# Levels 4 to 6 of a blocked triangular inverse on 32 or 64 columns a head instead of 128, its transpose written by VectorE's 32x32 transposes, in a decoder-layer kernel

## Chip, cores and metric

One core of a Trainium2 chip. The metric is the device time of one execution in microseconds (us); lower is better. TensorE is called PE in the profile's rows, VectorE DVE, ScalarE ACT, GpSimd POOL.

## What is computed

One layer of a hybrid decoder for 1,024 prompt tokens and 32 sample tokens, in float32 throughout: RMSNorm, one input projection (1024 to 3,592 columns), a gated DeltaNet branch (4 heads of 128) beside a short gated convolution, an output projection, a squared-ReLU MLP of width 4096, a gated embedding and a last norm. The change lies in the DeltaNet branch, in the triangular solve of each chunk of tokens:

```python
kk = jnp.einsum("bhnid,bhnjd->bhnij", k, k)
a_mat = jnp.eye(c, dtype=jnp.float32) + jnp.where(strict, beta[..., :, None] * kk * decay, 0.0)
rhs = jnp.concatenate([v * beta[..., None], k * (beta * jnp.exp(g))[..., None]], axis=-1)
sol = lax.linalg.triangular_solve(a_mat, rhs, left_side=True, lower=True, unit_diagonal=True)
u, w = sol[..., :dv], sol[..., dv:]
qk = jnp.einsum("bhnid,bhnjd->bhnij", q, k) * decay
```

The kernel takes chunks of 128 tokens and forms the inverse of the unit lower triangular 128x128 matrix of each head explicitly.

## The kernel before

**Two kinds of TensorE work in one order.** Every dense product is cut into groups of 352 columns (a third of the 1,056 tokens): 24 matmuls of 128x128 weights by 352 columns in a round-robin of three PSUM banks (`pg`). A product's operands are split into a high and a low part (`fp32r`), so that three matmuls stand for one. In the mixer stage the instructions of the recurrence are threaded between those of the input projection. The table `ORDER` is a list of steps `name chunk level n`: all engines walk the same list; at each step an engine does its share of that step, and TensorE then issues `n` matmuls of the projection (`fill`, line 815; here called **fills**). `vector_work` and `thirds` place VectorE's, ScalarE's and GpSimd's work on the projection (the copy out of a bank at line 1600 or 1744, the split of a weight panel into `w_hi` and `w_lo`, the convolution taps of line 1623, the silu) behind the step in whose fills the group ends. So a step's place in the list decides what each in-order engine has to do ahead of it. 72 fills are one projection unit (three groups of 24); the list holds 1,464 fills before the end and 48 behind it.

**The inverse.** There are eight chunks `c` of 128 tokens, worked in pairs (the even one in buffers 0, the odd in 1). `kk` makes the matrix (VectorE into `AT`), `kq` the query matrix. `b1` to `b4` invert the 16x16 diagonal blocks on VectorE in both, `b4` having GpSimd spread the 32x32 diagonal blocks of the transposed inverse into `XT`, and `turned` transposes it back into `X` (line 1853). Then level 4, 5 and 6 double the block size from 16 to 128, each in two steps: `y` is `LY` (the masked matrix, made by GpSimd) times `X` (line 872), ScalarE copies it out of PSUM; `z` is `XT` times that copy (line 886), and VectorE subtracts it from `X` (line 1858). The transpose is kept up at level 4 by a transpose of the whole `X` (line 1861), and at levels 5 and 6 by a second product (line 890) that is subtracted from `XT` (line 1863). All of these matmuls have 128x128 float32 weights and 128 moving columns; one program matmul of float32 is two records in the trace, so four heads are 8 records.

**After the inverse.** `vturn` turns v (ScalarE scales it out of PSUM), and `into`, `kturn`, `solve`, `update`, `sum`, `norm`, `scale` carry the state. The steps that begin with `s_` do the same for the 32 sample tokens between the first pair and the second. Three of them matter here:

- `s_y`: TensorE waits for `so_copied` 3, ScalarE's copy of the third `s_conv` product; it then multiplies the states with 8 moving columns (line 842), as `s_z` and `s_state` do.
- `s_onorm`: a small norm; ScalarE takes its Ln and Exp.
- `s_put`: the first one waits for `q_act` 13, which is that Ln.

Units 13 to 16 of the projection hold z: where one ends, ScalarE splits a weight panel, loads a table, applies silu (which waits for VectorE's copy of the group) and loads the table back.

## Time and profile before

| | |
|---|---|
| median of 3 runs (lowest to highest) | 1499.04 us (1497.4 to 1499.92) |
| the profiled execution | 1499.39 us, span 1497.6 us |
| TensorE | 98% of the span busy, 9,324 matmul records |
| VectorE, ScalarE, GpSimd | 49%, 32%, 17% |
| mean granted TensorE clock | 0.992 of full |

The span runs from the first to the last instruction; the execution's time has some 1.8 us around it. The mixer stage with the recurrence lies at about 118 to 515 us.

### The profile page before, as it was taken

The numbers are of one execution on the slowest core, as the hardware profiler recorded it, in microseconds if no ns is written. First come the engines' busy times: TensorE is split into PE (matmuls) and PEld (weight loads), VectorE is DVE, ScalarE is ACT, GpSimd is POOL, SyncE is SP. The second block draws the span as 40 slices with busy tenths as digits, with TensorE's granted clock in tenths as the row PEclk, the third lists the DMA queues.
The fourth block names the chain that finished last, engine by engine and source line by source line (L and its number), as shares of the span: only waits on it lengthen the run. The fifth ranks groups of instructions, "written<-read, shape, count | busy, mean of one in ns | idle before, by whom it ended". The sixth has DMA issues, their size and how long they took to land.

```text
span 1497.6 us, 24674 instructions
## 1 busy us (share of the span) xinstructions
PE 1463.6 (98%) x9324; PEld 1437.9 (96%) x9324; DVE 729.3 (49%) x1313; ACT 476.9 (32%) x856; POOL 248.2 (17%) x306
## 2 busy tenths in 40 slices
PE   7999999999999999999999999999999999999997
PEld 6999998999999899999999999999999999998997
DVE  5678844658584733633333333333433333335525
ACT  6324343332424322632131220312213122135525
POOL 3200312154343733000000000000000000040303
PEclk9999999999999999999999999999999999999999
DMA  7112313312213353111111111111111111112102
GB/s 178 44 43 58 99 34 99 92 40 71 72 45 106 64 117 84 32 55 42 42 43 57 43 43 43 54 44 43 43 56 42 43 43 56 43 42 72 29 29 116
DMA packets 166315, 89.83 MB, mean 60 GB/s; under 512 B 50763, under 2 KB 160267, under 8 KB 166230
## 3 DMA queue, kind: packets, MB, share of 16 engines
q1 hardware_dynamic: 165222, 84.89, 20.6%
q0 software_dynamic: 1008, 3.79, 0.6%
q8 instruction: 55, 0.90, 0.2%
q14 instruction: 30, 0.25, 0.1%
HBM read 77.97 MB, written 10.69 MB: 59 GB/s over the span
## 4 chain that ended last, share of the span: by engine, by line
PE 89%; DVE 4%; issue 2%; POOL 1%; ACT 1%; DMA 0%; DVEq 0%; POOLq 0%; SPq 0%
PE pg L696 65%; PE pg L815 14%; PE bk L872 1%; DVE act_lo L1975 1%; PE bk L890 1%; PE bk L886 1%; POOL act_lo L2296 1%; PE bk L842 1%; PE bk L1023 1%; DVE cv L1623 0%; PE bk L856 0%; PE bk L903 0%; PE bk L935 0%; PE bk L923 0%; PE bk L932 0%
## 5 line engine op out<-in xcount | busy, mean ns | idle before, releaser
L696 PE MATMUL pg<-act_hi,w_hi 128*128 128x352 f32 x1320 | 428.3, 325 | 8.0 <-issue 3.5
L696 PE MATMUL pg<-act_lo,w_hi 128*128 128x352 f32 x1320 | 424.5, 322 | 0.0
L696 PE MATMUL pg<-act_hi,w_lo 128*128 128x352 f32 x1296 | 416.1, 321 | 0.0
L696 PEld LDWEIGHTS pg<-act_hi,w_hi 128*128 128x128 f32 x1320 | 248.6, 188 | 11.1 <-issue 7.2
L696 PE MATMUL pg<-u_hi,w_hi 128*128 128x352 f32 x768 | 249.3, 325 | 0.0
L696 PEld LDWEIGHTS pg<-act_lo,w_hi 128*128 128x128 f32 x1320 | 249.2, 189 | 0.0
L696 PE MATMUL pg<-u_hi,w_lo 128*128 128x352 f32 x768 | 248.9, 324 | 0.0
L696 PE MATMUL pg<-u_lo,w_hi 128*128 128x352 f32 x768 | 247.8, 323 | 0.0
L696 PEld LDWEIGHTS pg<-act_hi,w_lo 128*128 128x128 f32 x1296 | 243.5, 188 | 0.0
L1152 ACT ACTIVATE w_hi<-w_raw 128x1024 fp32r<-128x1024 f32 x111 | 117.0, 1054 | 383.2 <-PE pg L696 319.8
L2337 POOL TENSOR_TENSOR ssq<-ssq,sq 128x352 f32<-128x352 f32 x72 | 76.2, 1067 | 875.3 <-ACT sq L1152 874.6
L2036 DVE TENSOR_TENSOR xres<-xres,pg 128x352 f32 (+1 forms) x192 | 99.2, 520 | 201.0 <-PE pg L696 201.0
L815 PE MATMUL pg<-act_hi,w_hi 128*128 128x352 f32 x504 | 167.1, 332 | 2.6 <-DVE pre L1600 2.6
L1543 DVE TENSOR_TENSOR w_lo<-w_raw,w_hi 128x1024 fp32r<-128x1024 f32 x110 | 138.6, 1260 | 58.4 <-ACT w_hi L1152 58.2
L815 PE MATMUL pg<-act_hi,w_lo 128*128 128x352 f32 x504 | 166.2, 330 | 0.0
L815 PE MATMUL pg<-act_lo,w_hi 128*128 128x352 f32 x504 | 165.5, 328 | 0.0
L696 PEld LDWEIGHTS pg<-u_hi,w_hi 128*128 128x128 f32 x768 | 145.0, 189 | 0.0
L696 PEld LDWEIGHTS pg<-u_lo,w_hi 128*128 128x128 f32 x768 | 144.5, 188 | 0.0
L696 PEld LDWEIGHTS pg<-u_hi,w_lo 128*128 128x128 f32 x768 | 143.9, 187 | 0.0
L1152 ACT ACTIVATE sq<-tm 128x352 f32<-128x352 f32 x96 | 47.8, 498 | 231.6 <-DVE tm L2022 231.6
L2026 DVE TENSOR_TENSOR u_lo<-sq,u_hi 128x352 f32 x96 | 50.5, 526 | 129.8 <-ACT u_hi L1152 129.8
L815 PEld LDWEIGHTS pg<-act_hi,w_hi 128*128 128x128 f32 x504 | 95.9, 190 | 5.4 <-DVE pre L1600 2.9
(331 smaller groups left out, 1643.8 us busy)
## 6 DMA issues: line engine op xcount, KB each, us to landing
w_raw<-in_w_up SPq DMA_DIRECT2D x32, 512.0 KB, 4.0
w_raw<-in_w_down SPq DMA_DIRECT2D x32, 512.0 KB, 3.4
w_raw<-in_w_in SPq DMA_DIRECT2D x29, 512.0 KB, 4.1
x_tok<-in_x_prompt SPq DMA_DIRECT2D x8, 512.0 KB, 8.0
w_raw<-in_w_out SPq DMA_DIRECT2D x8, 512.0 KB, 4.3
x_col<-in_x_prompt SPq DMA_DIRECT2D x32, 128.0 KB, 2.8
w_raw<-in_w_ple_gate SPq DMA_DIRECT2D x8, 512.0 KB, 4.1
out<-y_tok SPq DMA_DIRECT2D x8, 512.0 KB, 2.9
```

What stands on the lines that cost most here:

```text
L696: last = mm(pg[bank][:, 0:TH], w, a, start=i == 0, stop=i == len(terms) - 1)
L815: last = mm(pg[n][:, 0:TH], w, (act_hi, act_lo, act_hi)[r][:, k, cols(n)], start=k == 0 and r == 0, stop=k == KD - 1 and r == 2)
L842: last = mm(bk[4][:, c:c + 8], S_in[:, h, i, :], F0[:, c:c + 8], start=True, stop=True)
L872: per_head(lambda h, v: mm(A[x][:, v], LY[x][:, h, :], X[x][:, h, :], start=True, stop=True)) \
L886: last = per_head(lambda h, v: mm(A[x][:, v], XT[s][x][:, h, :], LY[x][:, h, :], start=True, stop=True))
L890: last = per_head(lambda h, v: mm(bank[:, v], LY[x][:, h, :], XT[s][x][:, h, :], start=True, stop=True))
L1023: mm(bk[c % 4][:, :], F0[0:TS, c // 2 * P:(c // 2 + 1) * P], by_seq[c % 4][0:TS, :, :], start=True, stop=True).then_inc(sm.q_pe, 1)
L1152: return nc.scalar.activation(out, in_, func, **kw)
L1543: tt(w_lo[b % 2][:, :, :], w_raw[b % 2][:, :, :], w_hi[b % 2][:, :, :].bitcast(f32), SUB) \
L2026: tt(rows(u_lo[c % 2][:, k, cols(n)]), sq[g % 2][:, :], rows(u_hi[c % 2][:, k, cols(n)]).bitcast(f32), SUB).then_inc(sm.u_lo_made, 1)
L2036: tt(x_t, x_t, pg[g % 3][:, 0:TH], ADD).then_inc(sm.evacuated, 2)
L2337: tt(ssq[:, cols(n)], ssq[:, cols(n)], sq[g % 2][:, :], ADD).then_inc(sm.ssq_added, 1)
```

## The change

The inverse is no longer held as a full 128x128 square for each head. At level 4 and 5 only its diagonal 32x32 blocks (32 columns a head, `narrow`) are multiplied, at level 6 its 64x64 blocks (64 columns a head, `pairs`). So `y` and `z` keep their 128x128 weights (`LY`, `XT`) and move 32 or 64 columns. The second product of levels 5 and 6 is gone: the new blocks of the transposed inverse are written straight into `XT` by VectorE's 32x32 block transposes, at level 6 after ScalarE has negated the product. Level 6 has one product before and after. The `turned` step is replaced by one transpose in `b4`. The masked matrix of the next level is made by GpSimd after `y` instead of after `z`, the rows of the next pair are loaded after `y` of level 6, and the fill counts in `ORDER` are all new; their sum is the same.

```diff
@@ z, y and kq on TensorE @@
                 elif k == "kq":
...
-                    if c > 1:
-                        pe.wait_ge(sm.x_updated, upd(c // 2 * 2 - 1, SQUARE))
...
                 elif k == "y":
                     pe.wait_ge(sm.lt_made, lev(c, l))
                     if l == BASE:
-                        pe.wait_ge(sm.x_copied, c + 1)
+                        pe.wait_ge(sm.x_copied, c // 2 + 1)
                     else:
-                        pe.wait_ge(sm.x_updated, upd(c, l - 1, l - 1 < SQUARE))
-                    per_head(lambda h, v: mm(A[x][:, v], LY[x][:, h, :], X[x][:, h, :], start=True, stop=True)) \
+                        pe.wait_ge(sm.x_updated, upd(c, l - 1, 1 if l == BASE + 1 else 2))
+                    src = pairs(x) if l == LEVELS - 1 else narrow(x)
+                    out = columns(A[x][:, half_cols(l)[0]], wide(l))
+                    per_head(lambda h, v: mm(out[:, h, :], LY[x][:, h, :], src[:, h, :], start=True, stop=True)) \
                         .then_inc(sm.y_mm, 1)
                 elif k == "z":
...
-                    if l < LEVELS - 1:
-                        last = per_head(lambda h, v: mm(A[x][:, v], XT[s][x][:, h, :], LY[x][:, h, :],
-                                                        start=True, stop=True))
-                    if l >= SQUARE:
-                        bank = A[2] if l == SQUARE else A[x]
-                        last = per_head(lambda h, v: mm(bank[:, v], LY[x][:, h, :], XT[s][x][:, h, :],
-                                                        start=True, stop=True))
-                    last.then_inc(sm.z_mm, 1)
+                    src = y_copy(x, l)
+                    out = columns(A[x][:, half_cols(l)[1]], wide(l))
+                    per_head(lambda h, v: mm(out[:, h, :], XT[s][x][:, h, :], src[:, h, :], start=True, stop=True)) \
+                        .then_inc(sm.z_mm, 1)
@@ ScalarE @@
                 elif k == "y":
                     act.wait_ge(sm.y_mm, lev(c, l))
-                    op(LY[x][:, :, :], heads(A[x]), ACT.Copy).then_inc(sm.ycopy_made, 1)
+                    if l == LEVELS - 1:
+                        act.wait_ge(sm.x_updated, upd(c, l - 1))
+                    op(y_copy(x, l), columns(A[x][:, half_cols(l)[0]], wide(l)), ACT.Copy).then_inc(sm.ycopy_made, 1)
+                elif k == "z" and l == LEVELS - 1:
+                    act.wait_ge(sm.z_mm, lev(c, l))
+                    op(negated(x)[64:P], A[x][64:P, half_cols(l)[1]].rearrange("p (a b j) -> p a b j", a=2, b=2), ACT.Copy, scale=-1.0) \
+                        .then_inc(sm.c_negated, 1)
@@ VectorE @@
+                    nc.vector.transpose(X[0][:, 0:2, :], X[1][:, 0:2, :]).then_inc(sm.x_copied, 1)
-                elif k == "turned":
-                    dve.wait_ge(sm.xt_made, c + 1)
-                    nc.vector.transpose(flat(X[x]), flat(XT[s][x])).then_inc(sm.x_copied, 1)
                 elif k == "z":
-                    xt = XT[s][x]
-                    dve.wait_ge(sm.z_mm, lev(c, l))
+                    xt, low, both = XT[s][x], narrow(x), pairs(x)
                     if l < LEVELS - 1:
-                        tt(X[x][:, :, :], X[x][:, :, :], heads(A[x]), SUB).then_inc(sm.x_updated, 1)
-                    if l < SQUARE:
-                        dve.wait_ge(sm.x_updated, upd(c, l, False))
-                        nc.vector.transpose(flat(xt), flat(X[x])).then_inc(sm.x_updated, 1)
+                        dve.wait_ge(sm.z_mm, lev(c, l))
+                        product = columns(A[x][:, half_cols(l)[1]], wide(l))
+                    if l == BASE:
+                        tt(low, low, product, SUB).then_inc(sm.x_updated, 1)
+                        dve.wait_ge(sm.x_updated, upd(c, l, 1))
+                        for g in range(GROUPS):
+                            f = slice(32 * g, 32 * g + 32)
+                            nc.vector.transpose(xt[f, :, f], low[f]).then_inc(sm.x_updated, 1)
+                    elif l == BASE + 1:
+                        dve.wait_ge(sm.xt_made, c // 2 * 2 + 2)
+                        stt(both[:, :, 0:32], low, m_grp[:, GROUPS:GROUPS + 1], product, MUL, SUB).then_inc(sm.x_updated, 1)
+                        ts_(both[:, :, 32:64], low, m_grp[:, GROUPS + 1:GROUPS + 2], None, MUL).then_inc(sm.x_updated, 1)
+                        dve.wait_ge(sm.x_updated, upd(c, l, 2))
+                        for g in (0, 2):
+                            f = slice(32 * g, 32 * g + 32)
+                            n = slice(32 * g + 32, 32 * g + 64)
+                            nc.vector.transpose(xt[f, :, n], both[n, :, 0:32]).then_inc(sm.x_updated, 1)
                     else:
-                        tt(xt[:, :, :], xt[:, :, :], heads(A[2] if l == SQUARE else A[x]), SUB).then_inc(sm.x_updated, 1)
+                        dve.wait_ge(sm.c_negated, c + 1)
+                        for g in range(2):
+                            for j in range(2):
+                                f = slice(32 * j, 32 * j + 32)
+                                n = slice(64 + 32 * g, 96 + 32 * g)
+                                nc.vector.transpose(xt[f, :, n].rearrange("p (a b) j -> p a b j", a=2), negated(x)[n, :, :, f]) \
+                                    .then_inc(sm.x_updated, 1)
@@ the order table, one line of it @@
-y 0 5 9; y 1 5 0; z 0 5 34; z 1 5 26; y 0 6 18; y 1 6 0; z 0 6 18; z 1 6 7;
+y 0 5 25; y 1 5 20; z 0 5 0; z 1 5 15; y 0 6 5; y 1 6 19; z 0 6 0; z 1 6 33;
```

**TensorE, levels 5 and 6 of the second pair.** Before (line 872 is y, 886 and 890 the two products of z, 912 `kturn`, 923 and 831 `solve` with the old state, 932 `update`; `bk` is a PSUM bank of the recurrence, `pg` one of the fills):

```order
L872 MATMUL bk<-X,LY 128x128 x4
L912 MATMUL bk<-ident,qkv 128x128 x4
L886 MATMUL bk<-LY,XT 128x128 x4
L890 MATMUL bk<-XT,LY 128x128 x4
L815 MATMUL pg<-act_lo,w_hi 128x352
L815 MATMUL pg<-act_hi,w_lo 128x352
L923 MATMUL bk<-rv,XT 128x128 x4
L831 MATMUL bk<-qkv,S 128x128 x4
L886 MATMUL bk<-LY,XT 128x128 x4
L890 MATMUL bk<-XT,LY 128x128 x4
L932 MATMUL bk<-wn,ktok 128x128 x4
L872 MATMUL bk<-X,LY 128x128 x4
```

After (893 is y, 903 z, 935 and 852 `solve`, 944 `update`):

```order
L893 MATMUL bk<-X,LY 128x32 x4
L903 MATMUL bk<-X,XT 128x32 x4
L935 MATMUL bk<-rv,XT 128x128 x4
L852 MATMUL bk<-qkv,S 128x128 x4
L903 MATMUL bk<-X,XT 128x32 x4
L836 MATMUL pg<-act_hi,w_lo 128x352
L836 MATMUL pg<-act_hi,w_hi 128x352
L836 MATMUL pg<-act_lo,w_hi 128x352
L836 MATMUL pg<-act_hi,w_lo 128x352
L944 MATMUL bk<-wn,ktok 128x128 x4
```

A z of level 5 is 4 matmuls of 32 columns now, and was 8 of 128.

**ScalarE, the sample steps up to s_y.** `X<-bk 27x512` is the copy of the second `s_conv` product, `PT<-bk 27x512` here that of the third, `w_hi`, the two table loads and `cv<-cv` the work at the end of a z unit, `PT<-bk 32x128` the copy in `s_y`. Before:

```order
L1152 ACTIVATE X<-bk 27x512
L1152 ACTIVATE X<-bk 32x128
L1152 ACTIVATE PT<-bk 27x512
L1152 ACTIVATE PT<-bk 32x128
L1152 ACTIVATE w_hi<-w_raw 128x1024
L1152 ACT_TABLE_LOAD
L1152 ACTIVATE cv<-cv 128x1056
L1220 ACT_TABLE_LOAD
L1152 ACTIVATE PT<-bk 32x512
L1152 ACTIVATE LY<-LY 128x128
L1152 ACTIVATE LY<-bk,eps 128x128
L1152 ACTIVATE LY<-LY 128x128
```

After, from the same copy on:

```order
L1164 ACTIVATE X<-bk 27x512
L1164 ACTIVATE X<-bk 32x128
L1164 ACTIVATE w_hi<-w_raw 128x1024
L1164 ACT_TABLE_LOAD
L1164 ACTIVATE cv<-cv 128x1056
L1232 ACT_TABLE_LOAD
L1164 ACTIVATE PT<-bk 27x512
L1164 ACTIVATE PT<-bk 32x128
L1164 ACTIVATE PT<-bk 32x512
L1164 ACTIVATE LY<-LY 128x128
```

The unit's work stood behind the third copy and stands ahead of it. TensorE has 12 fills between the third `s_conv` and `s_y` now, 8 before. The fills of these two pieces are in the table: before `s_conv 2 8; s_y 8`, after `s_xt 9; s_conv 2 12; s_y 10`.

**ScalarE, the norm and the first s_put.** `LY<-bk,eps` is the Ln of `s_onorm`. In the piece of before it directly follows the square `LY<-LY`. After:

```order
L1164 ACTIVATE LY<-LY 128x128
L1164 ACTIVATE w_hi<-w_raw 128x1024
L1164 ACT_TABLE_LOAD
L1164 ACTIVATE cv<-cv 128x1056
L1232 ACT_TABLE_LOAD
L1164 ACTIVATE LY<-bk,eps 128x128
```

The next z unit's end has moved ahead of the Ln. The fills: before `s_solve 29; s_out 0; s_onorm 26; s_put 0`, after `s_solve 18; s_out 15; s_onorm 17; s_put 0`.

## Rows read from the trace of the kernel before

**Rows 1.** The page: span, TensorE's share, the chain that ended last by engine.

```profile
span 1497.6 us, 24674 instructions
PE 1463.6 (98%) x9324; PEld 1437.9 (96%) x9324; DVE 729.3 (49%) x1313; ACT 476.9 (32%) x856; POOL 248.2 (17%) x306
...
PE 89%; DVE 4%; issue 2%; POOL 1%; ACT 1%; DMA 0%; DVEq 0%; POOLq 0%; SPq 0%
```

**Rows 2.** Windows: busy us of each engine (instructions), PEclk granted, DMA share, GB/s.

```profile
282.00:507.00 225.00, 224.78 (x1615) 220.50 (x1614) 150.96 (x335) 80.56 (x179) 96.58 (x91) 1.00 0.24 67
163.50:166.80 3.30, 3.30 (x13) 3.30 (x13) 3.30 (x7) 0.00 (x0) 3.30 (x4) 0.50 0.00 0
228.30:231.70 3.40, 3.40 (x37) 3.34 (x36) 0.36 (x1) 2.77 (x3) 0.60 (x1) 1.00 0.55 140
231.75:238.45 6.70, 6.70 (x29) 6.36 (x29) 0.67 (x5) 0.59 (x1) 0.00 (x0) 0.50 0.21 85
```

**Rows 3.** Who ended TensorE's waits, 120 to 520 us: total us, times, longest.

```profile
PE pg L815 <- DVE pre L1600: 2.6, 1, 2.6
...
PE bk L856 <- issue: 1.5, 1, 1.5
PE bk L1015 <- ACT LY L1152: 1.0, 1, 1.0
PE bk L959 <- ACT X L1152: 0.6, 1, 0.6
PE bk L864 <- issue: 0.2, 1, 0.2
```

**Rows 4.** TensorE's timeline in the second pair: start us, us, operands, records.

```profile
313.03 1.05 PE L872 MATMUL bk<-X,LY 128*128 128x128 f32 x8
313.92 0.60 PE L912 MATMUL bk<-ident,qkv 128*128 128x128 f32 x4
314.36 1.06 PE L886 MATMUL bk<-LY,XT 128*128 128x128 f32 x8
315.25 1.06 PE L890 MATMUL bk<-XT,LY 128*128 128x128 f32 x8
316.06 0.41 PE L815 MATMUL pg<-act_lo,w_hi 128*128 128x352 f32 x1
```

**Rows 5.** TensorE's timeline around s_y.

```profile
223.58 0.33 PE L815 MATMUL pg<-act_lo,w_hi 128*128 128x352 f32 x1
223.74 1.85 PE L842 MATMUL bk<-LY,S_in 128*128 128x8 f32 x16
225.52 0.43 PE L983 MATMUL bk<-X,AT 32*32 32x32 f32 x8
225.88 0.43 PE L815 MATMUL pg<-act_hi,w_lo 128*128 128x352 f32 x1
```

**Rows 6.** VectorE's timeline at the end of b3 and b4.

```profile
159.86 0.69 DVE L1776 TENSOR_REDUCE W<-X 128x64 f32<-128x512 f32 x1
160.58 0.74 DVE L1848 TENSOR_SCALAR X<-W,m_half 128x256 f32<-128x256 f32 x2
161.36 1.03 DVE L1849 STREAM_TRANSPOSE X<-X 128x512 f32<-128x512 f32 x1
162.49 0.53 DVE L1600 TENSOR_TENSOR pre<-pg,r_b 128x352 f32<-128x352 f32 x1
```

**Rows 7.** ScalarE's timeline: third s_conv copy, a z unit's end, the Ln.

```profile
222.65 0.59 ACT L1152 ACTIVATE PT<-bk 27x512 f32<-27x512 f32 x1 [0.62 <-PE bk L959]
...
226.34 1.06 ACT L1152 ACTIVATE w_hi<-w_raw 128x1024 fp32r<-128x1024 f32 x1
227.42 1.28 ACT L1152 ACT_TABLE_LOAD   x1
228.71 1.08 ACT L1152 ACTIVATE cv<-cv 128x1056 f32<-128x1056 f32 x1
229.81 1.28 ACT L1220 ACT_TABLE_LOAD   x1
...
247.33 0.37 ACT L1152 ACTIVATE LY<-bk,eps 128x128 f32<-128x128 f32 x1 [0.58 <-PE bk L1015]
```

**Rows 8.** VectorE's timeline from s_out on.

```profile
246.33 4.62 DVE L1954 TENSOR_TENSOR S_in<-S_in,XT 128x1024 f32<-128x1024 f32 x4
250.87 0.28 DVE L1958 TENSOR_TENSOR qkv<-LY 128x128 f32<-128x128 f32 x1
251.11 0.52 DVE L1744 TENSOR_TENSOR cv<-pg,r_b 128x352 f32<-128x352 f32 x1
```

**Rows 9.** TensorE's timeline at s_out and s_onorm.

```profile
244.69 1.07 PE L1010 MATMUL bk<-XT,AT 32*128 32x32 f32 x8
246.81 0.49 PE L1015 MATMUL bk<-LY,ones 128*128 128x128 f32 x2 [1.05 <-ACT LY L1152]
247.05 0.41 PE L815 MATMUL pg<-act_lo,w_hi 128*128 128x352 f32 x1
```

More of the change, by code:

```diff
@@ L76 @@
-norm 7 0 0; scale 7 0 0; tail 0 0 0
+begin 0 0 0; diff 0 0 8; diff 1 0 0; kk 0 0 79; kk 1 0 38; b1 0 0 17; b2 0 0 22; kq 0 0 44; b3 0 0 0; kq 1 0 5;
+b4 0 0 50; y 0 4 0; y 1 4 7; z 0 4 4; z 1 4 35; y 0 5 25; y 1 5 20; z 0 5 0; z 1 5 15; y 0 6 5; y 1 6 19;
+z 0 6 0; z 1 6 33; s_wait 0 0 0; s_begin 0 0 42; s_norm 0 0 17; s_conv 0 0 0; s_kk 0 0 18; s_conv 1 0 0;
+s_xt 0 0 9; s_conv 2 0 12; s_y 0 0 10; s_z 0 0 0; s_state 0 0 6; s_turn 0 0 4; s_solve 0 0 18; s_out 0 0 15;
+s_onorm 0 0 17; s_put 0 0 0; s_put 1 0 8; s_put 2 0 0; s_put 3 0 10; s_put 4 0 0; s_put 5 0 11; s_put 6 0 0;
@@ new lines @@
+s_put 7 0 45; vturn 0 0 0; vturn 1 0 0; diff 2 0 0; diff 3 0 3; kk 2 0 0; kq 2 0 0; kk 3 0 0; into 0 0 29;
+kq 3 0 0; b1 2 0 11; b2 2 0 20; kturn 0 0 18; b3 2 0 0; solve 0 0 33; b4 2 0 0; update 0 0 0; sum 0 0 14;
+y 2 4 0; y 3 4 0; into 1 0 0; z 2 4 0; z 3 4 16; norm 0 0 12; y 2 5 0; kturn 1 0 3; y 3 5 0; z 2 5 0;
+solve 1 0 0; z 3 5 4; update 1 0 9; sum 1 0 9; y 2 6 2; y 3 6 0; norm 1 0 0; scale 0 0 0; scale 1 0 7; z 2 6 0;
+z 3 6 10; vturn 2 0 13; diff 4 0 0; vturn 3 0 0; diff 5 0 0; kk 4 0 35; kk 5 0 0; kq 4 0 17; into 2 0 0;
@@ new lines @@
+kq 5 0 0; b1 4 0 22; b2 4 0 0; kturn 2 0 8; b3 4 0 2; solve 2 0 32; b4 4 0 0; update 2 0 0; sum 2 0 13;
+y 4 4 0; y 5 4 0; into 3 0 0; z 4 4 0; z 5 4 11; norm 2 0 5; y 4 5 5; kturn 3 0 0; y 5 5 0; z 4 5 0;
+solve 3 0 0; z 5 5 3; update 3 0 8; sum 3 0 2; y 4 6 0; y 5 6 11; norm 3 0 0; scale 2 0 0; scale 3 0 0;
+z 4 6 21; z 5 6 17; vturn 4 0 0; vturn 5 0 0; diff 6 0 0; diff 7 0 18; kk 6 0 0; kk 7 0 0; kturn 4 0 36;
+into 4 0 0; b1 6 0 21; solve 4 0 0; kq 6 0 0; b2 6 0 32; update 4 0 0; sum 4 0 0; kq 7 0 0; b3 6 0 0;
@@ L77 @@
+b4 6 0 27; into 5 0 0; norm 4 0 20; y 6 4 0; y 7 4 0; kturn 5 0 0; z 6 4 25; z 7 4 23; solve 5 0 6; y 6 5 0;
+y 7 5 0; update 5 0 0; z 6 5 0; z 7 5 23; sum 5 0 0; y 6 6 0; y 7 6 18; norm 5 0 0; scale 4 0 0; scale 5 0 6;
+z 6 6 0; z 7 6 21; vturn 6 0 0; vturn 7 0 0; into 6 0 11; kturn 6 0 5; solve 6 0 2; update 6 0 0; sum 6 0 13;
+into 7 0 0; kturn 7 0 0; norm 6 0 13; solve 7 0 17; update 7 0 0; sum 7 0 0; scale 6 0 34; norm 7 0 0;
+scale 7 0 0; tail 0 0 0
 """
@@ L500, in lev, with upd, wide, half_cols @@
             return 2 * (LEVELS - BASE) * (c // 2) + 2 * (l - BASE) + c % 2 + 1
-        def upd(c, l, both=True):
-            pair = 4 * (SQUARE - BASE + 1) + 2
-            if l == LEVELS - 1:
-                return pair * (c // 2) + pair - 2 + c % 2 + 1
-            return pair * (c // 2) + 4 * (l - BASE) + 2 * (c % 2) + (2 if both else 1)
+        def upd(c, l, part=None):
+            parts = {4: 5, 5: 4, 6: 4}
+            first = sum(2 * parts[j] for j in range(BASE, l)) + parts[l] * (c % 2)
+            return 2 * sum(parts.values()) * (c // 2) + first + (part or parts[l])
+        def wide(l):
+            return 64 if l == LEVELS - 1 else 32
+        def half_cols(l):
+            w = H * wide(l)
+            y = 256 if l == BASE + 1 else 0
+            return slice(y, y + w), slice(y + w, y + 2 * w)
+        def narrow(x):
+            return X[0][:, x, :].rearrange("p (h j) -> p h j", h=H)
+        def pairs(x):
+            return X[1][:, 2 * x:2 * x + 2, :].rearrange("p a (b j) -> p (a b) j", b=2)
+        def y_copy(x, l):
+            return pairs(x) if l == LEVELS - 1 else X[0][:, 2 + x, :].rearrange("p (h j) -> p h j", h=H)
+        def negated(x):
+            return view(X[0], P * x, (2 * P, 2), (64, 2), (1, 64))
+        def columns(ap, w):
+            return ap.rearrange("p (h j) -> p h j", j=w)
         def view(buf, offset, *dims):
@@ L628, in _ @@
                         .then_inc(sm.ge_in, 16)
[L629 to L630 removed]
+                elif k == "y" and l == LEVELS - 1 and 2 <= c < NTT - 2:
+                    sp.wait_ge(sm.y_mm, lev(c, l))
                     load_rows(c + 2)
```

44 lines of the change are left out of this document (10 added, 34 removed).

## Prediction

> **What bounds the kernel.** I read the page first: the span, TensorE's share of it, and the chain that ended last. TensorE is busy for 98% of the span and holds 89% of the chain [rows 1]. A part of the change is therefore worth what it does to TensorE's own queue, and an operation of another engine costs nothing until TensorE waits for it. The windows come next. From 282 to 507 us, where three of the four pairs are worked, TensorE is busy for 224.78 of 225 us at the full clock; VectorE has 33% to spare there, ScalarE 64% [rows 2]. The list of waits then says how little TensorE waits between 120 and 520 us: 2.6 us once for a bank that VectorE had not copied out, 1.5 us for `kk` 2, 1.0 at `s_onorm`, 0.6 at the third `s_conv`, 0.2 at a `kq` [rows 3]. Two stretches in that region run at the half clock, 3.4 and 6.8 us long [rows 2]. So there are three accounts: TensorE's work, its waits, and the clock.
>
> **1. TensorE's work.** What does a narrow matmul cost? With 128 moving columns the 8 records of line 872 start at 313.03 and the next group at 313.92: 0.89 us, 111 ns a record; lines 886 and 890 the same [rows 4]. With 8 moving columns on 128x128 weights, 16 records take 223.74 to 225.52: again 111 ns [rows 5]. The weights are what these two rows share, so the moving columns are free below 128, and all of `y` and `z` keep their 128x128 weights. I take 111 ns for 32 and 64 columns. The lower bound is the next row: 32x32 weights, 8 records in 0.36 us, 45 ns [rows 5]; it needs narrow weights, which this change doesn't have.
>
> The Trainium skill has a rule that speaks for a larger gain: in "TensorE: Matmul & The Clock Gate", section "Back-to-back issue gap", a matmul of 1 to 64 columns costs about 60 cycles, or 62 ns where the sequencer decodes. By that the 384 remaining records would each be some 50 ns cheaper, an estimate of 19 us more. The 8-column row disagrees, and the same page's section on LDWEIGHTS, where the time goes by weight columns, is with the row.
>
> What does go is the second product of level 5: 8 chunks x 4 heads x 2 records = 64 records x 111 ns = **-7.1 us**. The other groups stay, 24 `y` and 24 `z`, and the sum of fills is unchanged.
>
> **2. The wait at 160 us.** TensorE stands 2.6 us for a bank because `b3` and `b4` keep VectorE until 162.49, and only then is the group copied out [rows 3, 6]. Behind the wait the clock is halved: 13 records start in 3.3 us where 160 ns each would need 2.1, so 1.2 us more are lost [rows 2, 5]. The new table brings `kk` 0 forward to fill 8 and puts `b3` at fill 208, behind the group that ends at fill 192. The next group ends at fill 216 and its bank is asked for at fill 264: 48 fills, 7.7 us, while VectorE has what is left of `b3` and `b4`, about 5 us. The bank is free in time: **-3.8 us** (bounds: 0 if VectorE is as late elsewhere, -4.3 if the whole half-clock stretch, half of 3.4, is counted).
>
> **3. Waits that go.** `s_conv` 2 now has 9 fills (1.4 us) ahead of it: -0.6. `s_onorm` has 15 (2.4 us) after `s_out`: -1.0. The `kq` wait of 0.2 goes too. Together **-1.8 us** [rows 3]. The 1.5 us at `kk` 2 stay: `vturn` stands 20 fills instead of 13 behind the unit's end, but 3 fills instead of 10 follow it.
>
> **4. Waits that come.** Both are ScalarE's in-order queue around the end of a z unit. That block is 226.34 to 231.09: panel split, table, silu, table, 4.75 us [rows 7].
>
> *At `s_y`.* Before, the third copy stood ahead of it; now it stands behind. The block starts 0.46 us after the unit's last fill has started (225.88 and 226.34) [rows 5, 7], so the copy of 0.59 is done 5.8 us after that fill, a little later for the two copies ahead. TensorE needs 9 fills, `s_conv` 2 and 12 fills, 1.45 + 0.45 + 1.95 = 3.85 us. It waits **+2.1 us**. Queued behind the wait are the state products and all fills; nothing else runs on TensorE.
>
> *At the first `s_put`.* It waits for the Ln, which now stands behind the next block; and the silu in that block waits for VectorE's copy of the group, which stands behind four multiplications of `S_in`. From the start of `s_out` (244.69): those begin at +1.64 and end at +6.2, the group's copy at +6.6 [rows 8, 9]; silu 1.08, table 1.28, Ln 0.37 [rows 7] give +9.4. TensorE is there after 0.9 + 15 fills + 0.25 + 17 fills and two switches, +6.5. **+2.9 us** (bounds for both waits together: 0, if something in my order is off, to 6.5).
>
> **5. The clock.** Two rows show what precedes a fall: a wait of 2.6 us [rows 3], and 3.4 us of 8-column records without a pause [rows 2]. The new wait at `s_y` is followed by 1.8 us of 8-column records, so I expect one more half-clock stretch, over 10 fills: +1.5. The wait at `s_put` is like the one at 160 us: 1.2 us at perhaps three in four, +1.0. Together **+2.5 us** (bounds 0 and 3.4, two stretches at half of 3.4 each).
>
> **6. At no cost.** VectorE does one subtraction of 128 columns and four transposes at level 4 for two operations of 512, similar at 5 and 6; ScalarE gains a negation at level 6. I went through every step from the second pair on, with the fills between a product and its reader. The tightest are `update` 2 (about 0.6 us to spare after `b3`) and `norm` 6 (0.3 us). They are hidden by fills; if the cover is gone in all of them, it costs 1 to 2 us. After level 6 of chunk 3, `vturn` 2 waits for a negation and four transposes, some 1.5 us, and has 10 fills.
>
> **Sum.** 1499.4 - 7.1 - 3.8 - 1.8 + 2.1 + 2.9 + 2.5 = **1494.2 us**. The profiled execution is 1499.39, 0.35 above the median of the runs, which I leave inside the range.
>
> **Rivals.**
>
> *A, the sum above (0.58).* Its own range 1491 to 1497.5, by the clock's and `s_put`'s bounds.
>
> *B, the two ScalarE waits don't appear (0.14).* Something in the sample steps is late already and covers them, with the clock's part. Then -12.7 us alone, 1486.7; with one of them 1490. Against: the order of ScalarE's rows and the duration of the block are both plain.
>
> *C, narrow matmuls let the clock fall, a little (0.20).* A record of 32 columns lies between 8 columns, behind 3.4 us of which the clock was halved [rows 2], and 128, of which any number ran at full clock (282 to 507). The table puts four groups of 32 columns close together in four places, with one of 128 between (level 4 of each pair: y, y, into, z, z), some 4.5 us each. Each fall costs 1.2 to 1.7 us, since all around is TensorE's bound. Two to four falls: 1497 to 1501. The same page of the Trainium skill, section "HAM oscillation", has kernels with short matmul bursts fall to the half clock again and again; this trace shows it for 8 columns and pauses alone.
>
> *D, the same, in more than five places, level 6 too (0.05).* From five falls on, 1494.2 + 5 x 1.6 = 1502.2, slower than before; at all eight level stretches 1507. Against: the clock would have to fall although 128-wide groups and fills stand between.
>
> *E, a narrow matmul is cheaper (0.03).* At 45 ns a record, 384 x 66 ns = 25 us less: 1469.
>
> **How the numbers follow.** 0.2% is 3.0 us, about what a measurement of this kernel tells from no change; faster means under 1496.0. A lies under that by nine tenths (0.52), B and E wholly (0.17): 0.69. C and the rest of A make 0.26 for no change, D 0.05. The range leaves out E, D and the lower half of B: 1489 to 1500.
>
> **What would show it.** The forms of TensorE: y and z at 111 ns a record from start to start, 384 of them; the wait for `pre` at 160 us gone; a wait of 2 us ahead of line 863's first group and of 3 us ahead of the first `s_put`, both ended by ScalarE; PEclk 1.00 from the second pair on. A clock under 1 between 290 and 500 us speaks for C or D. What would make it wrong: VectorE late at a place that I took as covered, or a pace of narrow records that isn't 111 ns.

## The result and the profile after

The changed kernel takes **1506.34 us** (median of 19 runs, 1500.85 to 1511.12) against 1498.82 us (median of 19, 1496.52 to 1507.88) of the kernel before on the same chip: ratio **1.0038, 95% interval 1.0026 to 1.0050**. The prediction was 1494.2 in a range of 1489 to 1500, and faster. It was wrong in sign and outside its range. The profiled execution took 1505.23 us.

The page of the kernel after: span, busy time, the chain by engine. They answer to [rows 1].

```profile
span 1503.5 us, 24634 instructions
PE 1465.2 (97%) x9260; PEld 1435.9 (96%) x9260; DVE 738.2 (49%) x1375; ACT 472.5 (31%) x864; POOL 247.1 (16%) x306
...
PE 91%; DVE 2%; issue 2%; POOL 1%; ACT 1%; DMA 0%; DVEq 0%; POOLq 0%; SPq 0%
```

The trace has 64 TensorE records fewer, as it should, and yet TensorE is busy for 1.6 us more: some of its records take longer. The chain is still TensorE's. The waits of the mixer, 110 to 520 us, against [rows 3]:

```profile
PE bk L1035 <- issue: 3.0, 1, 3.0
PE bk L863 <- ACT PT L1164: 1.9, 1, 1.9
PE bk L877 <- issue: 1.5, 1, 1.5
PE pg L1064 <- POOL act_lo L2332: 1.1, 1, 1.1
```

Line 1035 is the first `s_put`, 863 the state product of `s_y`, 877 `kk` 2. The waits at 160 us, at the third `s_conv`, at `s_onorm` and at `kq` are gone; the two that were forecast have come, at 3.0 and 1.9 us. The windows, against [rows 2] (columns as there):

```profile
163.50:166.80 3.30, 3.30 (x27) 3.30 (x26) 3.27 (x3) 0.60 (x3) 2.87 (x4) 1.00 0.02 5
207.90:224.00 16.10, 14.16 (x110) 12.95 (x108) 4.45 (x13) 8.02 (x14) 2.80 (x6) 1.00 0.30 99
224.10:244.50 20.40, 20.40 (x99) 19.42 (x99) 1.19 (x6) 0.85 (x2) 0.00 (x0) 0.50 0.10 26
244.55:258.10 13.55, 10.53 (x68) 9.79 (x66) 8.53 (x11) 5.63 (x7) 4.62 (x5) 1.00 0.06 9
258.25:271.75 13.50, 13.50 (x27) 7.44 (x26) 3.52 (x6) 0.00 (x0) 4.12 (x4) 0.50 0.48 149
290.00:510.00 220.00, 220.00 (x1569) 215.92 (x1568) 156.99 (x391) 77.08 (x185) 94.44 (x91) 1.00 0.25 68
```

Here is the loss. Half clock of 3.4 us at 163 is gone, but 20.5 us stand from 224.1 to 244.5 and 13.7 from 258.2 to 271.8: 34.1 us at the half clock in the mixer, against 3.4 + 6.8 = 10.2 before. TensorE has no pause in either stretch (20.40 of 20.40 us, 13.50 of 13.50), and from 290 us on, among all the narrow products of the other three pairs, the clock is full.

TensorE's timeline at the start of the two stretches:

```profile
220.71 0.32 PE L836 MATMUL pg<-act_lo,w_hi 128*128 128x352 f32 x1
222.97 2.55 PE L863 MATMUL bk<-LY,S_in 128*128 128x8 f32 x16 [1.94 <-ACT PT L1164]
225.45 0.63 PE L995 MATMUL bk<-X,AT 32*32 32x32 f32 x8
226.01 0.66 PE L836 MATMUL pg<-act_hi,w_lo 128*128 128x352 f32 x1
...
229.11 3.42 PE L863 MATMUL bk<-LY,S_in 128*128 128x8 f32 x16
...
254.59 0.32 PE L836 MATMUL pg<-act_hi,w_lo 128*128 128x352 f32 x1
257.93 1.79 PE L1035 MATMUL bk<-AT,LY 32*128 32x512 f32 x2 [3.02 <-issue]
259.51 1.91 PE L1035 MATMUL bk<-X,LY 32*128 32x512 f32 x2
```

Each fall of this profile comes within 1.2 us of the end of a wait, and what follows the wait is lean: 16 records of 8 columns, or `s_put` products that use 32 of the 128 rows. 16 records of 8 columns take 3.42 us at the half clock and 1.85 at the full one [rows 5]; two `s_put` records start 1.6 to 1.9 us ahead of the next two, against 0.96 at full clock (245.54 and 246.50 in spread_products, a run of below). ScalarE's timeline ahead of both waits:

```profile
217.48 1.04 ACT L1164 ACTIVATE w_hi<-w_raw 128x1024 fp32r<-128x1024 f32 x1
218.54 1.28 ACT L1164 ACT_TABLE_LOAD   x1
219.84 1.09 ACT L1164 ACTIVATE cv<-cv 128x1056 f32<-128x1056 f32 x1
220.94 1.28 ACT L1232 ACT_TABLE_LOAD   x1
222.24 0.59 ACT L1164 ACTIVATE PT<-bk 27x512 f32<-27x512 f32 x1
...
255.06 1.08 ACT L1164 ACTIVATE cv<-cv 128x1056 f32<-128x1056 f32 x1 [0.87 <-DVE cv L1764]
256.17 1.28 ACT L1232 ACT_TABLE_LOAD   x1
257.46 0.37 ACT L1164 ACTIVATE LY<-bk,eps 128x128 f32<-128x128 f32 x1
```

The copy that `s_y` needs (222.24) and the Ln that `s_put` needs (257.46) both stand behind a z unit's block, as the order had it. Line 1035's releaser is printed as "issue"; the Ln that it waits for ends at 257.83, 0.1 us before it starts. And the narrow products in the second pair, against [rows 4]:

```profile
314.24 1.87 PE L893 MATMUL bk<-X,LY 128*128 128x32 f32 x16
315.94 1.14 PE L915 MATMUL bk<-S,qkv 128*128 128x128 f32 x8
316.92 1.87 PE L903 MATMUL bk<-X,XT 128*128 128x32 f32 x16
```

16 records of 32 columns take 1.70 us from start to the next group's start: 106 ns each, where 128 columns took 111.

### The profile page after: what moved, and what is told of

Its sections match the earlier page's. It is cut to its first block, busy times and chain, and to the rows that moved or that the text cites. A ratio compares the mean times of both kernels' runs of the same rounds, so it can differ in the third digit from the quotient of the medians.

```text
span 1503.5 us, 24634 instructions
## 1 busy us (share of the span) xinstructions
PE 1465.2 (97%) x9260; PEld 1435.9 (96%) x9260; DVE 738.2 (49%) x1375; ACT 472.5 (31%) x864; POOL 247.1 (16%) x306
## 4 chain that ended last, share of the span: by engine, by line
PE 91%; DVE 2%; issue 2%; POOL 1%; ACT 1%; DMA 0%; DVEq 0%; POOLq 0%; SPq 0%
PE pg L717 65%; PE pg L836 15%; PE bk L903 1%; PE bk L893 1%; DVE act_lo L2011 1%; PE bk L863 1%; PE bk L1035 1%; POOL act_lo L2332 1%; PE bk L877 0%; PE bk L935 0%; PE bk L883 0%; PE bk L915 0%; PE bk L944 0%; PE bk L947 0%; PE bk L952 0%
```

## What every run tells of the clock

Each run comes with its mean granted clock, so its time can be split: (1 - mean clock) x time is what the clock took, the rest is work and waits at full clock. Means over all runs of a kernel; those of the kernel before are the ones taken beside the experiments. The last column is the half clock between 110 and 500 us in the profiled execution (of two, where there are two).

| kernel | runs | clock took | the rest | half clock, us |
|---|---|---|---|---|
| before | 88 | 13.8 | 1487.0 | 10.2; 10.2 |
| after | 19 | 24.7 | 1481.5 | 34.1; 34.1 |
| old_sample_fills | 6 | 16.7 | 1477.4 | 17.1 |
| before_new_sample | 6 | 22.2 | 1490.6 | 27.3 |
| no_sy_wait | 10 | 19.5 | 1479.8 | 20.5 |
| no_sput_wait | 10 | 18.7 | 1479.0 | 23.9 |
| code_alone | 12 | 19.9 | 1483.4 | 23.9; 17.1 |
| first_pair_alone | 12 | 15.9 | 1489.1 | 10.2 |
| spread_products | 12 | 14.6 | 1477.9 | 0; 0 |
| wait_in_fills | 7 | 13.9 | 1480.1 | 17.1 |
| put_spread | 12 | 25.2 | 1480.3 | 44.4 |
| spread_more | 6 | 11.5 | 1481.1 | 3.4 |
| spread_and_cover | 6 | 10.2 | 1481.3 | 3.4 |
| onorm_cover | 12 | 13.7 | 1476.5 | 13.7 |

The standard error of a mean in the third column is 0.3 for the kernel before, 0.6 for that after, and 0.6 to 2.0 for the others. So the change took 5.5 us out of work and waits and put 10.9 into the clock. The 19 runs of the kernel before that stand beside the changed kernel's 19 come without clocks and can't be split; their mean is 1499.5 us, against 1500.8 in this table, so one of the two terms may be off by about 1 us.

## The experiments

The theory, called W below: the two new waits start half clocks, and the lean work behind them (8-column or 32-row products) holds the clock down. The first rival, N: the narrow products of the inverse leave the clock prone to fall, wherever. The 8-column products of `s_y`, `s_z` and `s_state` are called the state products. All edits are in the table of fills, whose sum stays the same; spread_products, spread_more, spread_and_cover and onorm_cover also let fills in between the state products, by an edit of the code.

**old_sample_fills**: the changed kernel with the sample steps' fills of before. Both waits go.

```diff
-s_begin 42; s_norm 17; s_conv0 0; s_kk 18; s_xt 9; s_conv2 12; s_y 10; s_state 6; s_turn 4; s_solve 18; s_out 15; s_onorm 17; s_put 0 8 0 10 0 11 0 45
+s_begin 16; s_norm 14; s_conv0 14; s_kk 25; s_xt 0; s_conv2 8; s_y 8; s_state 8; s_turn 5; s_solve 29; s_out 0; s_onorm 26; s_put 0 9 0 10 0 16 0 54
```

> The changed kernel with the sample steps' fills at the places of the kernel before (s_norm at fill 442, s_y at 503, s_out and s_onorm at 553, the first s_put at 579). Theory W (waits, then a held half clock): the two ScalarE waits of 1.9 and 3.0 us go, the 1.0 and 0.6 us of the kernel before come back, and the half clock between 210 and 290 us shrinks from 34 us to about 7: some 1505.2 - 3.3 - 12 = 1490 us, ratio to before 0.994. Rival N (the narrow matmuls ahead of the sample steps leave the clock prone to fall): the waits go but 15 to 30 us of half clock stay: 1498 to 1502. Rival O (waits alone, the clock stretches are by chance of the profiled run): 1502 in the median.

Measured: 1494.33 us (6 runs), ratio 0.9954 (0.9937 to 0.9971). The work and the waits came out as summed: -7.1 (records) -2.6 (the wait at 160) = -9.7 against before, 1487.0 - 1477.4 = 9.6 measured, with a standard error of 0.8. (That it fits to a tenth is luck: wait_in_fills, the same kernel but for 13 fills, gives 6.9.) The clock gave back 8.0 of its 10.9. But W had some 7 us of half clock in the sample steps and 1490 us, and the profile has 17.1 us there, as much as N asked for, in the state products, though no wait above 0.6 us is near:

```profile
221.40:238.30 16.90, 16.90 (x80) 15.92 (x80) 1.89 (x6) 4.50 (x5) 0.60 (x1) 0.50 0.21 65
238.50:262.00 23.50, 22.45 (x115) 17.52 (x114) 13.65 (x20) 5.70 (x7) 8.65 (x9) 1.00 0.33 99
```

So a wait is not needed for a fall in that stretch. The second row holds all of `s_put` but its end, without the wait: full clock.

**before_new_sample**: the kernel before with the changed kernel's sample fills, the same edit the other way round (`s_begin` 43, the last `s_put` 38).

> The kernel before, with its 128-wide inverse untouched, and the sample steps' fills at the places of the changed kernel. Theory W: waits of about 2 and 3 us come, and with them 25 to 35 us of half clock between 210 and 290 us: before + 13 to 17 us, ratio 1.009 to 1.011. Rival N: the waits come, but the half clock stays at 7 to 12 us, ratio 1.002 to 1.004.

Measured: 1512.28 us (6 runs), ratio 1.0081 (1.0064 to 1.0097). No narrow product is in it, and it has the same two waits (1.9 and 3.0 us), half clocks of 3.4 and 6.8 us in the state products and of 13.7 behind the wait at `s_put`:

```profile
238.10:244.80 6.70, 6.70 (x30) 6.36 (x30) 0.67 (x5) 0.13 (x1) 0.00 (x0) 0.50 0.00 0
258.60:272.20 13.60, 13.11 (x26) 7.44 (x26) 3.57 (x6) 0.69 (x3) 4.12 (x4) 0.50 0.49 144
```

Its clock took 8.4 us more than before. W had asked for a little more (a ratio of 1.009 to 1.011), N for much less (1.002 to 1.004). N is not the main cause: the fills of the sample steps are. They bring 8.4 of the 10.9 us without any of the changed code.

**no_sy_wait** and **no_sput_wait**: the changed kernel with one wait taken away each, by moving the step to the other side of the z unit's end.

```diff
 no_sy_wait
-s_kk 18; s_xt 9; s_conv2 12; s_y 10
+s_kk 10; s_xt 0; s_conv2 8; s_y 31
 no_sput_wait
-s_solve 18; s_out 15; s_onorm 17
+s_solve 9; s_out 0; s_onorm 41
```

> The changed kernel with s_xt, the third s_conv and s_y ahead of the unit's end at fill 504 (fills s_kk 10, s_xt 0, s_conv 2 8, s_y 31), nothing else moved. Theory W: the wait of 1.9 us is gone, the half clock before 250 us is 7 to 10 us instead of 20, the wait at the first s_put with its 13.7 us stays: about 1505.2 - 1.9 - 5 = 1498. Rival N: 1503, with the 20 us of half clock in place.

> The changed kernel with s_out and s_onorm ahead of the unit's end at fill 576 (fills s_solve 9, s_out 0, s_onorm 41), nothing else moved. Theory W: the wait of 3.0 us is gone, that of 1.0 at s_onorm is back, no half clock after 255 us, the first stretch of 20 us as before: about 1505.2 - 2.0 - 5.5 = 1498. Rival N: the second half-clock stretch stays, 1503.

Measured: 1499.38 (10 runs), ratio 0.9993 (0.9978 to 1.0008), and 1497.57 (10 runs), ratio 0.9982 (0.9969 to 0.9996). Without the first wait the clock took 5.2 us less than after, without the second 5.9 less (standard error about 1 each). Their windows, no_sy_wait first:

```profile
229.60:236.20 6.60, 6.60 (x28) 5.83 (x28) 0.67 (x5) 0.59 (x1) 0.00 (x0) 0.50 0.00 0
250.00:263.50 13.50, 13.50 (x27) 7.59 (x27) 3.57 (x6) 0.06 (x1) 4.12 (x4) 0.50 0.48 153
```

```profile
222.90:229.50 6.60, 6.60 (x34) 6.51 (x34) 0.53 (x1) 0.27 (x1) 0.00 (x0) 0.50 0.45 123
233.10:246.60 13.50, 13.50 (x55) 11.76 (x54) 2.19 (x8) 0.59 (x1) 2.19 (x3) 0.50 0.01 1
250.20:253.50 3.30, 3.30 (x13) 3.30 (x12) 2.93 (x4) 0.00 (x0) 0.00 (x0) 0.50 0.00 0
```

With the wait at `s_put` there are 13.7 us of half clock behind it; without it the `s_put` products run at full clock (the first starts at 257.22); the 3.4 us at 250 us lie among fills, behind a wait of 1.0 us at `s_onorm`.

**code_alone**: the changed code on the table of before, the `turned` steps' fills given to the step ahead.

> The changed kernel's code with the fill counts of before (the two turned steps of each pair dropped, their fills given to the step ahead). It separates the code from the table. If the sums of the prediction hold, TensorE loses 64 records of 111 ns, and the waits of before stay (2.6 us at 160 us with 3.4 us of half clock behind, 1.5 at kk 2, 1.0 at s_onorm, 0.6 at the third s_conv): 1498.8 - 7.1 = 1491.7 us, ratio 0.9953, and about 10 us of half clock between 110 and 520 us as in before. If the narrow products themselves make the clock prone to fall, there are more half-clock stretches in the mixer than before has, some of them in the inverse, and the time is 1495 or more. If the gain of the sample fills in the earlier experiment (ratio 0.9954) came with the new first pair (-3.8), this kernel should be 3.8 us slower than -10.9 would give; if the first pair is worth nothing, it equals that experiment, 1494.

Measured: 1503.35 us (12 runs), ratio 1.0014 (1.0002 to 1.0026). A miss by 12 us. The profile has new waits: 2.8 us at `vturn`, whose VectorE work had more fills ahead of it in the new table, 0.7 at `update`, 0.3 more at 160 us. -7.1 + 3.8 = -3.3; measured in the rest, -3.6. The narrow code needs its own table. The clock took 6.1 more than before, of which the half clock of 3.4 us behind the wait at `vturn` explains 1.7 in this profile.

**first_pair_alone**: the kernel before with the first pair's steps up to `b4` at the new places, the two `turned` steps at fill 243.

> The kernel before, with the first pair's steps from the start to b4 at the changed kernel's fills (kk 0 at fill 8, b3 at 208; the two turned steps behind b4). It tests the second term of the sum by itself: the wait of 2.6 us at 160 us and the 3.4 us of half clock behind it go, y 0 starts 3.8 us earlier (at about 164.6 us instead of 168.4), everything behind it is the same: 1495.0 us, ratio 0.9975. Rival: the later part of the mixer gets its time back at another wait, then 1498.8 with y 0 early all the same; or the clock takes it back in the sample steps, then a half clock longer than 6.8 us there.

Measured: 1504.10 us (12 runs), ratio 1.0026 (1.0010 to 1.0043). A miss by 9 us. The wait at 160 us went, but the old `turned` step waits for GpSimd's part of `b4`, and y 0 for it:

```profile
171.54 3.53 PE L872 MATMUL bk<-X,LY 128*128 128x128 f32 x16 [5.41 <-DVE X L1853]
174.83 0.41 PE L815 MATMUL pg<-act_hi,w_lo 128*128 128x352 f32 x1
```

So the new first pair leans on the new code, which writes that transpose within `b4`, and this kernel does not test the term alone. In old_sample_fills it stands beside the term for the records, and the two together come out. What this row is good for: a wait of 5.4 us, longer than any of after, with 128-column products and fills behind it, cost one half clock of 3.4 us (171.3 to 174.7).

**spread_products**: old_sample_fills with 8 fills between `s_z` and `s_state` and 8 between the latter's two halves.

```diff
-                    against_state(2)
+                    against_state(2)
+                    fill(a, a + 8)
+                    a += 8
                     against_state(3).then_inc(sm.q_pe, 1)
```

> The changed kernel with the sample steps' fills of before (the experiment that measured ratio 0.9954), and 16 more fills between the 8-column state products: 8 ahead of the products of s_state, 8 between its two halves, so that no 32 records of 8 columns stand together; the 16 are taken from behind the last s_put. Same work. If the half clock of 17.1 us that this stretch had in that experiment comes from the 8-column records that stand together, it is gone or at most 3.4 us long: -5 us or so against that experiment, 1489 us, ratio 0.992. If a lean mix is enough, or if it comes from something else (the pause of 0.5 us at the third s_conv, the small products of s_conv and s_kk ahead), the half clock stays and is longer, since more fills are in the stretch at half pace: 1494 to 1497.

**spread_again** is a second profile of it.

> The kernel of spread_products once more, for a second profile of it: its twelve runs fell in two groups, 1484 to 1489 us at a clock of 0.993 to 0.994 and 1495 to 1500 us at 0.985 to 0.989, and the profile shows one of the first. If the second group is a half clock in the sample steps that comes in some executions, a profile of 1495 us or more shows it there, 17 us or longer. If it lies elsewhere (the MLP, the end), the sample steps stay at full clock in it.

Measured: 1492.43 us (12 runs, 1484.29 to 1500.11), ratio 0.9940 (0.9917 to 0.9963); spread_again 1486.24. The runs fall in two groups: six at 1484.3 to 1489.5 with a clock of 0.993 or 0.994, six at 1495.4 to 1500.1 with 0.985 to 0.989. The median is not at the 1489 us that was expected, and the mean of what the clock took, 14.6 against 16.7 in old_sample_fills, differs by about its error. Both profiles are of the first group, and have no half clock in the sample steps at all (spread_again); no profile caught the second group:

```profile
205.00:270.00 65.00, 61.91 (x409) 54.01 (x408) 25.98 (x60) 24.48 (x39) 12.87 (x17) 1.00 0.34 102
```

**spread_more** (halves of 8 records with 6 fills behind each, 48 in all) and **spread_and_cover** (7 fills behind each `s_put` too, `kk` 2 ten fills later):

> The changed kernel with the sample steps' fills of before, and the 8-column state products in halves of 8 records with 6 fills behind each half (48 fills in that stretch, which had 32 when 16 records stood together and 16 in the version before that), taken from behind the last s_put. The experiment with 32 fills had two outcomes, six runs at a mean clock of 0.993 to 0.994 and six at 0.985 to 0.989. If records of 8 columns standing together make the falls, the lower outcome goes: all runs at 0.992 or more, 1487 to 1490 us, ratio 0.9915. If any lean stretch will do and more fills in it only make it longer, both outcomes stay, 1487 and 1497 us.

> The kernel of spread_more with the s_put products evened out too (7 fills behind each) and kk 2 ten fills later behind vturn (they are taken from behind into 0), so that its wait of 1.5 us goes. If the state products were all that made the falls in the sample steps, it is 1.5 us faster than spread_more, 1486 to 1488 us; if the s_put products share in them, the mean clock rises a little more; if kk 2 is the start of a chain (b1, b2) that is needed in time, its wait comes back at y of level 4 and nothing is gained.

Measured: 1492.77 (6 runs), ratio 0.9946 (0.9928 to 0.9964), and 1490.78 (6 runs), 0.9939 (0.9921 to 0.9957). The clock was 0.990 or more in all twelve runs, and what the clock took is the least of all, 11.5 and 10.2. The medians are some 3 us above the ranges that were expected. The gain against spread_products went into a wait: `s_onorm` has moved 32 fills and now stands behind a z unit's block, 2.7 us instead of 1.0, with one half clock of 3.4 us behind it (spread_more: the wait, then the window). In spread_and_cover the 1.5 us at `kk` 2 are gone, and 0.6 came at the `kq` behind it.

```profile
PE bk L1030 <- ACT LY L1167: 2.7, 1, 2.7
```

```profile
244.80:248.00 3.20, 3.20 (x13) 3.20 (x13) 3.20 (x2) 0.68 (x2) 3.20 (x3) 0.50 0.43 168
```

**onorm_cover**: spread_more with that wait taken away (`s_turn` 3, `s_solve` 14, `s_out` 6, so that the step stands ahead of the unit's end).

> The kernel of spread_more with 14 fills instead of 29 between s_solve and s_out and 6 instead of none behind s_out, so that s_onorm stands ahead of the z unit's end and has a cover; kk 2 is five fills later. The wait of 2.7 us at s_onorm (ended by ScalarE) and the 3.4 us of half clock behind it go if ScalarE's block was what it waited for: -2.7 - 1.7 against spread_more, 1488.5 us, ratio 0.992. If VectorE's part behind s_solve is late now, the wait moves to s_out and nothing is gained.

Measured: **1488.59 us** (12 runs, 1482.77 to 1501.32), ratio **0.9930 (0.9901 to 0.9958)**: the lowest median, 1488.5 was expected. The wait is gone. But the two groups are back: six runs at 0.994 or 0.995 (to 1486.15 us), six at 0.983 to 0.990 (from 1491.03 us). The median lies in the gap between them, so that it met the expectation is in part luck, and its interval overlaps those of the three kernels above. Its profile is of the second group:

```profile
205.00:227.10 22.10, 21.55 (x178) 20.70 (x176) 4.97 (x14) 10.22 (x17) 3.57 (x7) 1.00 0.30 87
227.30:240.80 13.50, 13.50 (x55) 13.07 (x54) 1.21 (x7) 0.47 (x1) 0.00 (x0) 0.50 0.05 22
241.00:270.00 29.00, 29.00 (x148) 22.44 (x148) 17.02 (x24) 8.25 (x10) 8.69 (x9) 1.00 0.34 100
```

In the 22.1 us ahead of that fall TensorE paused for 0.55 us in all. With 6 fills between 8 records of 8 columns a fall can still come, and once it had come it lasted for 13.7 us. The Trainium skill, "TensorE: Matmul & The Clock Gate", section "HAM oscillation — how this bites in real kernels", lays the falls that it describes to pauses between bursts of matmuls; this fall and that of old_sample_fills came without such a pause.

**put_spread**: the changed kernel, 9 fills behind each `s_put` instead of none and some by turns. The wait ahead stays.

> The changed kernel with nothing but the fills between the eight s_put products evened out: 9 behind each (11 behind the last) instead of none and 8 to 11 by turns, so that two 32-row products no longer stand together. The first of them stays where it is and so does the wait of 3.0 us ahead of it. If lean work behind a wait holds the half clock, the 13.7 us stretch behind that wait is shorter, 3.4 to 6.8 us: -3.5 to -5 us against the changed kernel, ratio to before about 1.001. If a half clock begun by such a wait has its length from the wait alone, the stretch stays 13.7 us and the ratio 1.0038.

Measured: 1506.17 us (12 runs), ratio 1.0028 (1.0010 to 1.0047), the clock took 25.2. A miss: the stretch behind the wait is not shorter but longer. The windows of both stretches, then the fifth of the eight `s_put` products:

```profile
225.30:249.00 23.70, 23.70 (x109) 22.18 (x110) 2.47 (x8) 0.85 (x2) 1.78 (x2) 0.50 0.09 23
259.50:279.80 20.30, 19.52 (x44) 12.20 (x44) 4.09 (x7) 0.97 (x3) 4.12 (x4) 0.50 0.32 93
```

```profile
279.96 1.12 PE L1035 MATMUL bk<-AT,LY 32*128 32x512 f32 x2
```

Evening out did not end the half clock sooner: it lasted for 20.5 us, through four products and their fills. But it ended at 279.8 us, and the other four products, with the same 9 fills between them, ran at full clock to 289 us. So the mix alone does not hold the clock down for as long as it lasts.

**wait_in_fills**: old_sample_fills with 13 fills moved from ahead of y at level 6 of the third pair to behind it, to make a wait among full-width work.

> The experiment with the sample steps' fills of before again, with the 13 fills that stood between z 5 at level 5 and y at level 6 moved behind y 5 of level 6, in the third pair. TensorE must then wait there for VectorE's two level-5 operations and transposes and for the update, some 2 to 4 us, in a region where all around is full-width fills and 128-column products. If a wait starts a half clock that full-width work ends soon, the profile shows the wait, then one stretch of 3.4 us at 0.50 (1.2 to 1.7 us lost), and the time is that experiment's 1494.3 plus 3 to 6. If any half clock lasts 13 us or more once begun, whatever runs, such a stretch is seen here too (6 to 10 us lost, over 1500). If a wait alone starts none, PEclk stays 1.00 there.

Measured: 1494.32 us (7 runs), ratio 0.9949 (0.9931 to 0.9968). Inconclusive: no wait came there but 0.2 us at `update`. Its profile has 17.1 us of half clock in the state products, as that of old_sample_fills. What a wait costs among full-width work is read from other runs (below).

**before_again**, **after_again**, **code_alone_again**: second profiles.

> The kernel before, a second profile. Over all runs it lost 13.8 us to the clock on average (one minus the mean clock, times the time), and its first profile 12. If its half clock in the sample steps is 6.8 us in most executions, a loss of 12 to 14 shows again two to three slices there; if executions differ by where the clock's slices fall, it may be 13 us or more there, or none.

> The changed kernel, a second profile. By the theory that the two waits start half clocks which the lean work behind them holds, it shows them again behind the waits of 1.9 and 3.0 us, 10 to 20 us each; by the rival that the narrow products of the inverse make the clock fall in some executions, a part of the half clock lies in 165 to 205 us or from 290 us on.

> The changed code on the fill counts of before, a second profile. It lost 19.9 us to the clock on average against 13.8 of before, of which the wait at vturn explains 1.7. If the rest comes from a longer half clock in the sample steps in most executions, this profile has again 13 us or more there, as its first (17.1); if that was the luck of one execution, it has 6.8 or less, and the rest lies elsewhere (behind new waits, at the end).

Measured: 1500.68, 1501.90 and 1501.79 us. The kernel before has 3.4 and 6.8 us at the same two places again, and 13.7 at its end. after_again:

```profile
222.60:229.20 6.60, 6.60 (x33) 6.51 (x34) 0.53 (x1) 0.27 (x1) 0.00 (x0) 0.50 0.46 124
232.80:246.30 13.50, 13.50 (x55) 12.14 (x55) 2.08 (x8) 0.59 (x1) 2.08 (x3) 0.50 0.00 1
256.70:270.20 13.50, 12.83 (x25) 7.38 (x26) 3.57 (x6) 0.87 (x3) 4.12 (x4) 0.50 0.51 141
290.00:500.00 210.00, 210.00 (x1509) 206.33 (x1509) 149.37 (x383) 72.77 (x174) 88.61 (x84) 1.00 0.22 66
```

34.1 us again, at the same two places, and none in the inverse. At the state products they come in two pieces now; the second begins 10 us behind the wait, with no pause ahead of it. code_alone_again has 6.8 us in the state products where its first profile had 17.1, so one kernel can have either. It has 3.4 us among fills behind the wait of 1.0 us at `s_onorm`, 6.8 behind the wait at 160 us, where the other had 3.4, and none behind the wait of 2.0 us at `vturn`. Outside 110 to 500 us the profiles of the kernel before have 15.3 and 24.0 us of half clock, those of the changed kernel 18.6 and 10.0: so what the changed kernel loses by the clock lies in the mixer.

## Why the prediction was wrong, step by step

**The step that failed is 5, the clock**, "one more half-clock stretch, over 10 fills: +1.5" and "the wait at `s_put` is like the one at 160 us: 1.2 us at perhaps three in four, +1.0". The number of stretches was right, their length was not. I took the 3.4 us of the row at 160 us as the size of a half clock, but that wait has fills behind it, and these two have lean work. My own rows spoke against it: the window at 231.75 us in rows 2, among the state products, is at the half clock for 6.7 us. (Nor are the 3.4 us ahead of it 8-column records alone: 8 records of 32x32 weights stand among them, from 229.03 us.) Put together, the stretches of the sample steps and the waits of 2 us or more, over all 18 profiles (without two stretches of 3.4 us among fills, behind waits of 1.0 us at `s_onorm`):

| what stands behind | the wait ahead | half clock that followed, us |
|---|---|---|
| fills or 128-column products | 2.0 to 5.4, ten times | 3.4 in eight, 6.8 in one, none in one (2.0) |
| `s_put`, 32 rows | 3.0, five times | 13.7 in four, 20.5 in one (put_spread) |
| `s_put`, 32 rows | none | none, in thirteen profiles |
| state products, 8 columns, 16 records and more together | 1.9, five times | 20.5 in three, 10.2 in one, 23.9 in one (put_spread) |
| the same | 0.6 at most | 6.8 in five, 17.1 in three |
| the same, with 8 or 6 fills between 16 or 8 records | 0.6 at most | none in four, 13.7 in one |

The term predicted at +2.5, or +1.3 with the 1.2 that step 2 had counted off, measured +10.9. Each wait taken away by itself gave back 5.2 and 5.9; both taken away (old_sample_fills) gave back 8.0, with an error of 1.3, so the two are not simply added. Put into the old code, the same fills brought 8.4. The fall at 160 us that went is -1.7, and the 4.2 that are left go with the changed code (see what stays open). That the wait starts the fall is shown at `s_put`: it came in five profiles of five with the wait and in none of thirteen without. At the state products the wait makes the half clock longer. That the work behind a wait sets the length rests on comparing places, 3.4 us behind fills and 13.7 behind `s_put`; no run puts full-width work behind one of these two waits, and put_spread shows that more fills between the lean products did not shorten it.

The other steps:

- **1, the work, -7.1**: right; 106 to 111 ns a record, 64 fewer, and the rest of the split time fits within its error in old_sample_fills.
- **2, the wait at 160 us, -3.8**: right. y 0 starts at 164.56 us where it started at 168.41: -3.85.
- **3, -1.8**: right; the waits are gone, `kk` 2 keeps its 1.5.
- **4, +2.1 and +2.9**: right, 1.9 and 3.0. From `s_out` (248.29) the Ln ended at +9.5, predicted +9.4.
- Steps 1 to 4 without their clock are -6.5; measured in the rest, -5.5. The missing 1 us may lie behind the mixer, where several short waits are longer (line 717 waits 2.3 us for `act_lo` in the profile after, 0.7 in that of before).
- **6, no cost elsewhere**: right for the new table (no wait over 0.2 us in the second to fourth pair but `kk` 2). With the old table the same code waits for 3.8 us.

Of the rivals, B and E did not occur. **C and D are refuted as put**, falls among the level groups: in all the profiles with narrow products none has a half clock between 290 and 500 us, but for the one behind the wait at `vturn` in code_alone. D had the right time, 1502 to 1507, by another mechanism. I gave the side "slower" 5% because I let the clock's term be bounded by 3.4 us.

**What stays open.** Some 4 us of clock go with the changed code and not with the fills of the sample steps: after took 24.7 and before_new_sample 22.2, though only the latter has the fall at 160 us (1.7); code_alone took 19.9 against 13.8, of which 1.7 at most is explained. The profiles place it, not in the inverse but in the state products behind it. With the fills of after, these have 10.2 us of half clock in the old code (one profile) and 20.5, 20.5, 20.5 and 23.9 in the changed one. With the fills of before they have 6.8 in all three profiles of the old code, and 17.1, 17.1, 17.1 and 6.8 in the changed one. So N is right in a weaker form: something in the changed code makes the half clock of the state products longer. What it is no run shows. Nor is it shown what decides between 17.1 and 6.8 us in one kernel, or between the two groups of runs.
